# A block-triangular inverse by four-quadrant products in a state-space mixer, and merged small operations in a differential attention

## The chip, the cores and the metric

The kernel runs on one core of a Trainium2 chip. The core has a matrix engine (PE, TensorE), three engines for elementwise work (DVE is VectorE, ACT is ScalarE, POOL is GpSimd) and a queue that only issues transfers (SP). They share an on-chip memory (SBUF) and the matrix engine's output memory (PSUM, here two rings of four banks, `psum_a` and `psum_d`). The metric is the device time of one launch in microseconds (us), lower is better.

## The reference

The program is one block of a hybrid model (512 tokens, width 1024) followed by two layers of another. The change touches two places. The first block has an RWKV-7 mixer of 16 heads, whose state is updated token by token:

```python
def step(state, inp):
    r_t, w_t, k_t, v_t, a_t, b_t = inp
    sa = jnp.einsum('bhvk,bhk->bhv', state, a_t)
    state = (state * w_t[:, :, None, :] + sa[..., None] * b_t[:, :, None, :]
             + v_t[..., None] * k_t[:, :, None, :])
    return state, jnp.einsum('bhvk,bhk->bhv', state, r_t)
```

It is followed by a group norm per head (`(y - mu) * rsqrt(var + GN_EPS) * gn_w + gn_b`). Each of the two later layers has a differential attention of four heads; the output's squares belong to the norm behind it:

```python
s = s - slopes[None, None, :, None, None] * dist[:, None, None]
p = jax.nn.softmax(s, axis=-1)
a = p[:, 0] - lam * p[:, 1]
return jnp.einsum('bhqk,bkhd->bqhd', a.astype(v.dtype), v)
```

## The kernel before

Every engine runs a program written out by hand, in order; semaphores couple them. Semaphores `full_a`/`full_d` say that a PSUM bank is written, `free_a`/`free_d` that it was read out. ACT reads the ring `a`, DVE the ring `d`. Weights come as 440 blocks of 128x1024 through SP; POOL splits each block into two fp32r parts when PE has used the block before the last, so POOL works in bursts that follow PE's dense products (L574, L577, L578: three per 128x128 weight tile).

**The RWKV stage** runs from about 270 to 871 us. Eight iterations j = 0 to 7 (`pe_rwkv`, `act_rwkv`, `dve_rwkv`) take two heads each (a pair: 64 channels in the lower and 64 in the upper partitions) and four chunks of 128 tokens. In each chunk the recurrence is solved by the inverse of a unit triangular matrix of 128x128. The kernel builds the inverse by doubling. Its two diagonal blocks of 64x64, for eight units u (two heads times four chunks), lie in `R_TN`, and its transpose in `R_TC`. Level 0 gives both from masks. Then levels k = 1 to 5 each do:

- PE, helper `blocks` (L1195): Z = L · TN, 16 products of 64x64, whose input rows and output partitions are the same half; DVE multiplies by the level's mask (L2516);
- PE: `normal` = TC · Z (16 products), DVE adds it to `R_TN` (L2532);
- PE: `last` = the transposed update (16 products), DVE adds it to `R_TC` (L2532 again).

Between them stand the steps of the chain of the iteration before (`PeChain`): per chunk `first` (L1097, L1099, output W), `second` (L1112, L1114, output U = T · W), `third` (L1125 to L1134, new state and output Y). ACT copies W, U and Y out of PSUM (L1695), DVE makes the new state (L2456 to L2466). In levels 2 and 4 PE also computes dense products for the next iteration (24 instructions), in level 3 one plain product. DVE's own inputs for the next iteration are spread over the levels (`dve_rwkv_input`, the reciprocal L2414 in level 4), and the group norm of iteration j - 2 (`dve_rwkv_normed` with reciprocal L2564, `dve_rwkv_mixed`) stands in level 2. Level 5 is followed by transposes (L729), masked maps (`pe_rwkv_maps`, L1157 and L1159, DVE L2477) and the corner block (L1203) that joins the two diagonal blocks. DVE then prepares the next iteration (`dve_rwkv_prepare`, L2431 to L2444), for which PE waits at L637 (`rk_ready`).

**The differential attention** (two layers, about 1658 to 1741 and 2730 to 2813 us) has 32 units, two per pair. For each unit DVE adds distances and takes the row maximum (L2672), negates it (L2677), ACT takes the exponential with its sum (L1877); for each pair DVE takes two reciprocals (L2689, L2691) and combines both halves (L2693, L2696), PE transposes (L729), ACT copies (L1886), PE multiplies by V (L797), DVE scales the output (L2703) and sums its squares (L2706). PE fills with halves of gate products (L759, L762, L763).

## Time and profile before

| | us |
|---|---|
| time before, median of 3 runs | 3494.92 |
| the runs | 3494.77 to 3496.0 |
| the profiled execution's own time | 3495.8 |
| its span (first to last instruction) | 3494.0 |
| outside the span | 1.8 |
| granted PE clock, mean | 0.98 |

The granted clock is a share of 2.4 GHz; in a stretch it is either near 1 or near 0.5 (1.2 GHz). In a timeline row the record of a PE group overlaps the next one by its pipeline's tail, so what a group costs is read from start to start. An fp32 product stands as two matmul records, so 16 products are x32. A bracket at a row's end is the idle time of that engine ahead of it and what ended it.

### The profile page before, as it was taken

To read this page: it belongs to the slowest core of one execution; us is meant where nothing else is said; L and a number is where in the kernel's file an instruction comes from. 1 tells how busy PE (TensorE), PEld (TensorE's weight loads), DVE (VectorE), ACT (ScalarE), POOL (GpSimd) and SP (SyncE) were. 2 spreads that over 40 slices of the span, in tenths; PEclk is the share of its full clock that TensorE was granted. 3 is DMA by queue.
4 is the path that set the end of the run, shared out by engine and by line. 5 is a ranking of instruction groups with operands and counts; after the bars stand their busy time and mean duration, and the time that the engine had idled before them with its cause. 6 is when DMAs were issued, how large, how long until landed. Compare 5 with 4: busy or idle time off the path is not lost.

```text
span 3494.0 us, 54483 instructions
## 1 busy us (share of the span) xinstructions
PE 3296.9 (94%) x20334; PEld 2615.5 (75%) x20334; DVE 2061.9 (59%) x2829; ACT 1019.0 (29%) x1866; POOL 1679.5 (48%) x1323
## 2 busy tenths in 40 slices
PE   7988999999999999989899899999989999999999
PEld 4766777777888888657778788887657677788887
DVE  4647777874566555541745575557551645576556
ACT  2152322222121112551435231113462435231112
POOL 3423222222657664225264566665326363666665
PEclk9999999999999999999999999999999999999999
DMA  5431111111323332112021233332102121223332
...
DMA packets 71664, 268.48 MB, mean 77 GB/s; under 512 B 7840, under 2 KB 7968, under 8 KB 68384
## 3 DMA queue, kind: packets, MB, share of 16 engines
...
q14 instruction: 60, 0.49, 0.0%
...
## 4 chain that ended last, share of the span: by engine, by line
PE 74%; DVE 19%; ACT 3%; issue 2%; DMA 1%; DVEq 0%; POOL 0%; SPq 0%; ACTq 0%; POOLq 0%
PE psum_a L574 10%; PE psum_a L577 10%; PE psum_a L578 10%; PE psum_d L574 5%; PE psum_d L577 4%; PE psum_d L578 4%; PE psum_d L637 4%; PE psum_d L1195 3%; PE psum_a L729 2%; PE psum_a L600 2%; PE psum_d L832 2%; PE psum_a L604 2%; PE psum_a L603 2%; DVE arena L2672 1%; PE psum_a L759 1%
## 5 line engine op out<-in xcount | busy, mean ns | idle before, releaser
L3274 POOL TENSOR_TENSOR w_lo<-raw,w_hi 128x1024 fp32r<-128x1024 f32 x440 | 1119.4, 2544 | 36.7
L3270 POOL TENSOR_TENSOR mark<-mark 128x1 f32<-128x1 f32 x438 | 105.5, 241 | 1738.4 <-PE psum_a L574 899.3
L574 PE MATMUL psum_a<-h_hi,w_hi 128*128 128x512 f32 x1712 | 675.2, 394 | 0.0
L577 PE MATMUL psum_a<-h_lo,w_hi 128*128 128x512 f32 x1712 | 667.4, 390 | 0.0
L578 PE MATMUL psum_a<-h_hi,w_lo 128*128 128x512 f32 x1712 | 667.4, 390 | 0.0
L3271 POOL TENSOR_SCALAR w_hi<-raw 128x1024 fp32r<-128x1024 f32 x440 | 471.2, 1071 | 33.7 <-DMA raw<-in_weights 33.7
L574 PEld LDWEIGHTS psum_a<-h_hi,w_hi 128*128 128x128 f32 x1712 | 322.1, 188 | 77.8 <-issue 11.2
L578 PEld LDWEIGHTS psum_a<-h_hi,w_lo 128*128 128x128 f32 x1712 | 322.0, 188 | 67.7
L577 PEld LDWEIGHTS psum_a<-h_lo,w_hi 128*128 128x128 f32 x1712 | 322.0, 188 | 67.4 <-issue 1.9
L574 PE MATMUL psum_d<-split,w_hi 128*128 128x512 f32 x848 | 331.2, 391 | 9.5 <-DVE x L3021 6.7
L577 PE MATMUL psum_d<-split,w_hi 128*128 128x512 f32 x848 | 330.0, 389 | 0.0
L578 PE MATMUL psum_d<-split,w_lo 128*128 128x512 f32 x848 | 330.0, 389 | 0.0
L574 PEld LDWEIGHTS psum_d<-split,w_hi 128*128 128x128 f32 x848 | 159.2, 188 | 47.2 <-issue 13.0
L578 PEld LDWEIGHTS psum_d<-split,w_lo 128*128 128x128 f32 x848 | 159.2, 188 | 33.1
L577 PEld LDWEIGHTS psum_d<-split,w_hi 128*128 128x128 f32 x848 | 159.2, 188 | 32.7
L637 PE MATMUL psum_d<-arena 64*128 64x512 f32 (+4 forms) x480 | 158.1, 566 | 12.1 <-DVEq L2819 6.9
L1195 PEld LDWEIGHTS psum_d<-arena 64*64 64x64 f32 x3840 | 123.9, 137 | 40.0 <-issue 14.2
L1195 PE MATMUL psum_d<-arena 64*64 64x64 f32 x3840 | 138.1, 224 | 15.2 <-DVE arena L2532 10.9
L759 PE MATMUL psum_a<-h_hi,w_hi 128*128 128x256 f32 x416 | 123.7, 297 | 0.0
L1841 ACT ACTIVATE arena<-arena,col 128x512 f32<-128x512 f32 (+5 forms) x144 | 104.3, 725 | 47.1 <-DVE col L2610 26.4
L763 PE MATMUL psum_a<-h_hi,w_lo 128*128 128x256 f32 x416 | 117.6, 283 | 0.0
L762 PE MATMUL psum_a<-h_lo,w_hi 128*128 128x256 f32 x416 | 117.6, 283 | 0.0
...
## 6 DMA issues: line engine op xcount, KB each, us to landing
raw<-in_weights SPq DMA_DIRECT2D x440, 512.0 KB, 3.6
...
```

Of the source, the lines that this page charges most:

```text
L574: m = pe.eng.matmul(dst, wh, hi(t), start=t == 0, stop=False)
L577: pe.eng.matmul(dst, wh, lo(t), start=False, stop=False)
L578: m = pe.eng.matmul(dst, wl, hi(t), start=False, stop=t == k - 1)
L637: pe.eng.matmul(tl.ps[0:lhsT.shape[1], 0:rhs.shape[1]], lhsT, rhs, start=True, stop=True)\
L759: m = pe.eng.matmul(tl.ps[:, cols], wh, b.h_hi[:, t, cols], start=t == 0, stop=False)
L762: pe.eng.matmul(tl.ps[:, cols], wh, b.h_lo[:, t, cols], start=False, stop=False)
L763: m = pe.eng.matmul(tl.ps[:, cols], wl, b.h_hi[:, t, cols], start=False, stop=t == KD - 1)
L1195: m = pe.eng.matmul(tl.ps[r, u * HD:(u + 1) * HD], lhsT(r, u), rhs[r, u], start=True, stop=True)
L1841: a.eng.activation(u.x, u.x, ACT.Exp, bias=u.neg, scale=1.0 if u.scale is None else u.scale, accum_out=u.sum)\
L3270: eng.tensor_tensor(b.mark[:, 1:2], b.mark[:, 0:1], b.mark[:, 0:1], ALU.add)
L3271: eng.tensor_scalar(hi, b.raw[:, s], 1.0, 0.0, ALU.mult, ALU.add).then_inc(sig["w_high"], 1)
L3274: eng.tensor_tensor(lo, b.raw[:, s], hi.bitcast(F32), ALU.subtract).then_inc(sig["w_ready"], 1)
```

## The change

- `products` takes the place of `blocks`: again 16 products of 64x64 per call, but a step through all four combinations of input half and output half, into two banks of ring `d`. The output blocks lie transposed against the input, so that Z is written with halves exchanged, and the second call brings them back.
- `R_TC` and its update are gone. Each level transposes `R_TN` (four 128x128 transposes, `inverse`), ACT copies it to `R_TW`, and the second product reads that. `diagonal` (16 products with the identity) gives the transposed diagonal blocks once, behind level 5.
- DVE's mask and add become two instructions each of half width (one per bank), 2 x 128x4x64.
- `second` of the chain reads one 128x128 matrix `R_TF` (its lower left zeroed in iterations 0 and 1): two products instead of four.
- In level 5 the second product stands ahead of the transposes and maps.
- `dve_rwkv_normed` of iteration j - 2 stands ahead of the levels, no longer in level 2.
- In the differential attention one negation and one reciprocal serve both units of a pair, ACT waits for `s_ready` once a pair, and the sum of squares is done by ACT (`act_output_square`).

```diff
         self.R_LM = ar(21, 8).rearrange("p (u m t) -> p u m t", u=8, m=4)
         self.R_Z, self.R_TN = (ar(a).rearrange("p (u t) -> p u t", u=8) for a in (29, 30))
-        self.R_TC = [ar(a).rearrange("p (u t) -> p u t", u=8) for a in (31, 32)]
-        self.R_T6 = [ar(a).rearrange("p (u t) -> p u t", u=8) for a in (33, 34)]
+        self.R_TW = self.plain[:, 6].rearrange("p (u t) -> p u t", u=8)
+        self.R_TF = [ar(a, 2).rearrange("p (u t) -> p u t", u=8) for a in (31, 33)]
         self.R_E = (self.col[:, 156:159], self.col[:, 172:175])
         self.R_WU = ar(35, width=1024).rearrange("p (s n) -> p s n", s=8)
         self.R_Y, self.R_YC, self.R_SQ, self.R_STD = (ar(n) for n in (37, 38, 41, 42))
...
         pe.eng.wait_ge(self.w.free, pe.taken(self.w))
         tl = pe.tile("a")
         pe.eng.wait_ge(tl.free, pe.emptied(tl))
-        upper, lower = ROWS
         for r, u in self.heads(c):
-            pe.eng.matmul(tl.ps[upper, r], self.TC[upper, u], self.W[upper, r], start=True, stop=True)
-        for r, u in self.heads(c):
-            m = pe.eng.matmul(tl.ps[lower, r], self.T6[:, u], self.W[:, r], start=True, stop=True)
+            m = pe.eng.matmul(tl.ps[:, r], self.TF[:, u], self.W[:, r], start=True, stop=True)
         m.then_inc(tl.full, pe.up("full_a"))
         self.u = tl
...
-    def blocks(lhsT, rhs):
+    def products(lhsT, rhs):
+        tiles = [pe.tile("d") for _ in range(2)]
+        pe.eng.wait_ge(tiles[1].free, pe.emptied(tiles[1]))
+        for v in range(4):
+            for n, (row, out) in enumerate(((0, 0), (1, 1), (0, 1), (1, 0))):
+                m = pe.eng.matmul(tiles[row].ps[ROWS[out], v * HD:(v + 1) * HD], lhsT(v, row, out), rhs(v, row, out),
+                                  start=True, stop=True)
+                if v == 3 and n >= 2:
+                    m.then_inc(tiles[row].full, pe.up("full_d"))
+        return tiles[1]
+
+    def block(t, v, row, out):
+        return t[ROWS[row], 2 * v + out]
+
+    def diagonal(src):
         tl = pe.tile("d")
         pe.eng.wait_ge(tl.free, pe.emptied(tl))
         for u in range(8):
             for r in ROWS:
-                m = pe.eng.matmul(tl.ps[r, u * HD:(u + 1) * HD], lhsT(r, u), rhs[r, u], start=True, stop=True)
+                m = pe.eng.matmul(tl.ps[r, u * HD:(u + 1) * HD], src[r, u], b.ident[r, r], start=True, stop=True)
         m.then_inc(tl.full, pe.up("full_d"))
         return tl
...
         else:
             pe.eng.wait_ge(normal.free, pe.taken(normal))
-        z = blocks(lambda r, u: LT[r, u, r], b.R_TN)
+        z = products(lambda v, row, out: LT[ROWS[row], 2 * v + out, ROWS[row]], lambda *at: block(b.R_TN, *at))
+        inverse = pe_turned(pe, [b.R_TN[:, 2 * v:2 * v + 2].rearrange("p u t -> p (u t)") for v in range(4)])
         if c is not None:
             chain.first(c)
         if k == 2 and more:
@@ -1222,27 +1234,26 @@
         if k == 5:
             if j:
                 pe_rwkv_mean(pe)
+        pe.eng.wait_ge(inverse.free, pe.taken(inverse))
+        pe.eng.wait_ge(z.free, pe.taken(z))
+        normal = products(lambda *at: block(b.R_TW, *at), lambda *at: block(b.R_Z, *at))
+        if k == 5:
             for src in (b.R_V, b.R_BH, b.R_KH):
                 turned = pe_turned(pe, [src[:, q * P:(q + 1) * P] for q in range(NQ)])
             pe_rwkv_maps(pe, j, (0, 1))
-        if k == 1:
-            pe.eng.wait_ge(pe.sem["t_ready"], pe.due("t_ready"))
-        pe.eng.wait_ge(z.free, pe.taken(z))
-        normal = blocks(lambda r, u: TC[r, u], b.R_Z)
         if c is not None:
             chain.second(c)
-        last = blocks(lambda r, u: b.R_Z[r, u], TC)
-        if c is not None:
             chain.third(c)
         if k == 3 and more:
             pe_rwkv_length(pe)
     upper, lower = ROWS
     pe.eng.wait_ge(normal.free, pe.taken(normal))
     z = corner(lower, lambda u: LT[upper, u, lower], lambda u: b.R_TN[upper, u])
+    last = diagonal(b.R_TN)
     maps = pe_rwkv_maps(pe, j, (2, 3))
     pe.eng.wait_ge(last.free, pe.taken(last))
     pe.eng.wait_ge(z.free, pe.taken(z))
-    last = corner(upper, lambda u: b.R_Z[lower, u], lambda u: b.R_T6[j % 2][lower, u])
+    last = corner(upper, lambda u: b.R_Z[lower, u], lambda u: TF[lower, u, HD:])
     if j:
         pe_rwkv_variance(pe)
     return PeChain(pe, j, (turned, maps, last))
...
@@ -1708,7 +1719,12 @@
     else:
         a.eng.wait_ge(a.sem["rk_ready"], KD)
         act_late_gate(a, 0)
-    for k in range(1, NQ + 1):
+    for k in range(1, NQ + 2):
+        a.eng.wait_ge(a.sem["full_a"], a.due("full_a"))
+        a.eng.activation(b.R_TW, a.bank().rearrange("p (u t) -> p u t", u=8), ACT.Copy).then_inc(a.sem["free_a"], a.up("free_a"))
+        if k > NQ:
+            continue
         if j:
             act_rwkv_chunk(a, W)
...
@@ -1869,7 +1885,8 @@
         if 0 <= s - 1 < n_units:
             u = units[s - 1]
-            a.eng.wait_ge(a.sem["s_ready"], a.due("s_ready"))
+            if s % 2:
+                a.eng.wait_ge(a.sem["s_ready"], a.due("s_ready"))
             if u.sink is not None:
                 a.eng.activation(u.sunk, u.sink, ACT.Exp, bias=u.neg).then_inc(a.sem["act_step"], a.up("act_step"))
@@ -1885,6 +1902,18 @@
                 a.eng.activation(u.pt[:, b0 * P:b0 * P + w], a.bank()[:, 0:w], ACT.Copy)\
                     .then_inc(a.sem["free_a"], a.up("free_a"))
+        if 0 <= s - lag - 3 and units[s - lag - 3].v:
+            act_output_square(a, units[s - lag - 3])
+    for u in units[-2:]:
+        if u.v:
+            act_output_square(a, u)
+
+
+def act_output_square(a, u):
+
+    a.eng.wait_ge(a.sem["o_written"], a.due("o_written"))
+    a.eng.activation(u.square[0], u.o, ACT.Square, accum_out=u.square[1]).then_inc(a.sem["act_step"], a.up("act_step"))
...
@@ -2225,6 +2253,9 @@
         u.inv, u.sunk = b.col[:, 124 + n % 4:125 + n % 4], b.col[:, 128 + n % 8:129 + n % 8]
         if u.neg_lam is not None:
             u.inv = b.col[:, n % 32:n % 32 + 1]
+        if n % 2:
+            u.two_top, u.two_inv = b.col[:, 119 + n % 4:121 + n % 4], b.col[:, n % 32 - 1:n % 32 + 1]
+            u.two_neg, u.two_sum = b.col[:, c - 2:c + 2:2], b.col[:, c - 1:c + 3:2]
     return units
...
+    eight, four = (lambda ps: ps.rearrange("p (u t) -> p u t", u=8)), (lambda ps: ps[:, 0:4 * HD].rearrange("p (v t) -> p v t", v=4))
+    every = lambda t, half: t.rearrange("p (v i) t -> p v i t", i=2)[:, :, half]
     for us in (slice(0, 4), slice(4, 8)):
         v.eng.wait_ge(v.sem["full_d"], v.due("full_d"))
@@ -2504,20 +2536,17 @@
             .then_inc(v.sem["free_d"], v.up("free_d"))
     v.eng.tensor_tensor(b.R_TN, b.R_TN, eye, ALU.add).then_inc(v.sem["t_ready"], v.up("t_ready"))
-    for r in ROWS:
-        v.eng.tensor_tensor(TC[r], b.R_LM[r, :, 0, r], low1t[r], ALU.mult).then_inc(v.sem["dve_step"], v.up("dve_step"))
-    v.eng.tensor_tensor(TC, TC, eye, ALU.add).then_inc(v.sem["t_ready"], v.up("t_ready"))
+    if j >= 2:
+        dve_rwkv_normed(v, j - 2)
     for k in range(1, 6):
-        level = v.each(b.const[:, C_LEVEL + (k - 1) * HD:C_LEVEL + k * HD], 8)
-        v.eng.wait_ge(v.sem["full_d"], v.due("full_d"))
-        v.eng.tensor_tensor(b.R_Z, eight(v.bank()), level, ALU.mult).then_inc(v.sem["free_d"], v.up("free_d"))
+        level = v.each(b.const[:, C_LEVEL + (k - 1) * HD:C_LEVEL + k * HD], 4)
+        for half in range(2):
+            v.eng.wait_ge(v.sem["full_d"], v.due("full_d"))
+            v.eng.tensor_tensor(every(b.R_Z, half), four(v.bank()), level, ALU.mult).then_inc(v.sem["free_d"], v.up("free_d"))
         if k == 2 and more:
             dve_rwkv_input(v, j + 1, 2)
         if k == 2 and j >= 2:
-            dve_rwkv_normed(v, j - 2)
             dve_rwkv_mixed(v, j - 2)
         if k == 4 and more:
             for step in (4, 8, 9):
@@ -2525,22 +2554,26 @@
         if k == 5:
             if j:
                 dve_rwkv_centered(v)
-            dve_rwkv_maps(v, (0, 1))
-        for dst in (b.R_TN, TC) if k < 5 else (b.R_TN,):
+        for half in range(2):
+            dst = every(b.R_TN, half)
             v.eng.wait_ge(v.sem["full_d"], v.due("full_d"))
-            v.eng.tensor_tensor(dst, dst, eight(v.bank()), ALU.add).then_inc(v.sem["free_d"], v.up("free_d"))
+            v.eng.tensor_tensor(dst, dst, four(v.bank()), ALU.add).then_inc(v.sem["free_d"], v.up("free_d"))
         if k == 5:
-            v.eng.wait_ge(v.sem["full_d"], v.due("full_d"))
-            ps, step = eight(v.bank()), "dve_step"
-            for r, dst in zip(ROWS, (TC, b.R_T6[j % 2])):
-                v.eng.tensor_tensor(dst[r], TC[r], ps[r], ALU.add).then_inc(v.sem[step], v.up(step))
-                step = "free_d"
+            dve_rwkv_maps(v, (0, 1))
         if j and k < NQ:
             dve_rwkv_state(v, j - 1, k - 1)
         if k in (1, 3) and more:
             dve_rwkv_input(v, j + 1, k)
+    if j < 2:
+        v.eng.memset(TF[HD:P, :, 0:HD], 0.0).then_inc(v.sem["dve_step"], v.up("dve_step"))
+    v.eng.wait_ge(v.sem["full_d"], v.due("full_d"))
+    ps, step = eight(v.bank()), "dve_step"
+    for r, cols in zip(ROWS, ROWS):
+        v.eng.tensor_copy(TF[r, :, cols], ps[r]).then_inc(v.sem[step], v.up(step))
+        step = "free_d"
     dve_rwkv_maps(v, (2, 3))
     if more:
         dve_rwkv_input(v, j + 1, 7)
@@ -2672,23 +2705,15 @@
                 v.eng.tensor_tensor_reduce(out=u.s[:, at:at + w], in0=v.bank()[:, 0:w], in1=m, scale=1.0, scalar=least, op0=ALU.add, op1=ALU.max, accum_out=u.top)\
                     .then_inc(v.sem["free_d"], v.up("free_d"))
                 at, least = at + w, u.top
-            if u.scale is None or u.dist is not None:
-                v.eng.tensor_scalar(u.neg, u.top, -1.0 if u.scale is None else -u.scale, None, ALU.mult)\
-                    .then_inc(v.sem["s_ready"], v.up("s_ready"))
-            else:
-                v.eng.tensor_scalar(u.neg, u.top, -1.0, u.scale, ALU.mult, ALU.mult)\
-                    .then_inc(v.sem["s_ready"], v.up("s_ready"))
-            if extra:
-                extra(s)
+            if s % 2:
+                v.eng.tensor_scalar(u.two_neg, u.two_top, -u.scale, None, ALU.mult).then_inc(v.sem["s_ready"], v.up("s_ready"))
         if 0 <= s - 2 < len(us) and us[s - 2].ready == "p_ready" and us[s - 2].v:
             u0, u1 = us[s - 3], us[s - 2]
             if base + s - 1 > 0:
                 v.eng.wait_ge(v.sem["e_done"], v.value("e_done", base + s - 1))
-            v.eng.reciprocal(u0.inv, u0.sum).then_inc(v.sem["dve_step"], v.up("dve_step"))
-            v.eng.reciprocal(u1.inv, u1.sum).then_inc(v.sem["dve_step"], v.up("dve_step"))
+            v.eng.reciprocal(u1.two_inv, u1.two_sum).then_inc(v.sem["dve_step"], v.up("dve_step"))
             v.eng.scalar_tensor_tensor(u1.inv, u1.inv, u1.neg_lam, u0.sum, ALU.mult, ALU.mult)\
...
@@ -2703,8 +2728,7 @@
                 v.eng.tensor_scalar(u.o, v.bank()[:, 0:u.width], us[s - lag - 2 - late_by].inv, None, ALU.mult)\
                     .then_inc(v.sem["free_d"], v.up("free_d"))
-                v.eng.tensor_tensor_reduce(out=u.square[0], in0=u.o, in1=u.o, scale=1.0, scalar=0.0, op0=ALU.mult, op1=ALU.add, accum_out=u.square[1])\
-                    .then_inc(v.sem["dve_step"], v.up("dve_step"))
+                v.eng.sem_inc(v.sem["o_written"], v.up("o_written"))
             else:
                 if u.sink is not None:
```

The engine PE in a middle iteration with a chain, level 1 up to its dense products. L1195 is `blocks`, L1099 `first`, L1112 and L1114 `second`, L1125 to L1134 `third`. Before:

```order
L1195 MATMUL psum_d<-arena 64x64 x16
L1099 MATMUL psum_a<-arena 128x64 x2
L1195 MATMUL psum_d<-arena 64x64 x16
L1112 MATMUL psum_a<-arena 64x64 x2
L1114 MATMUL psum_a<-arena 64x64 x2
L1195 MATMUL psum_d<-arena 64x64 x16
L1125 MATMUL psum_d<-arena 128x128
```

After, where L1192 is `products`, L729 the transposes of `inverse`, L1111 `second` and L1122 the start of `third`:

```order
L1192 MATMUL psum_d<-arena 64x64 x16
L729 MATMUL psum_a<-const,arena 128x128 x4
L1099 MATMUL psum_a<-arena 128x64 x2
L1192 MATMUL psum_d<-arena,plain 64x64 x16
L1111 MATMUL psum_a<-arena 128x64 x2
L1122 MATMUL psum_d<-arena 128x128
```

The third group of 16 between `second` and `third` is gone, four transposes stand behind the first group, and `second` has two instructions for four.

The engine DVE from the end of level 0 to level 1, iterations j >= 2. L2506 adds the unit diagonal to `R_TN`, L2509 and L2511 build `R_TC`. Before:

```order
L2506 TENSOR_TENSOR arena<-arena,const 128x512
L2509 TENSOR_TENSOR arena<-arena,const 64x512 x2
L2511 TENSOR_TENSOR arena<-arena,const 128x512
L2516 TENSOR_TENSOR arena<-psum_d,const 128x512
L2532 TENSOR_TENSOR arena<-arena,psum_d 128x512 x2
```

After, where L2597 and L2599 are `dve_rwkv_normed`:

```order
L2538 TENSOR_TENSOR arena<-arena,const 128x512
L2597 RECIPROCAL arena<-arena 128x512
L2599 SCALAR_TENSOR_TENSOR arena<-arena,par 128x512
L2546 TENSOR_TENSOR arena<-psum_d,const 128x4x64 x2
L2561 TENSOR_TENSOR arena<-arena,psum_d 128x4x64 x2
```

The reciprocal takes the place of the transposed copy's setup; mask and add are two halves each, and the second add is gone.

The engine DVE in level 2 of the same iterations: mask, shift of the next keys (L2729, L2731), group norm, add. Before:

```order
L2516 TENSOR_TENSOR arena<-psum_d,const 128x512
L2729 TENSOR_TENSOR arena<-arena 128x512
L2731 SCALAR_TENSOR_TENSOR arena<-arena,par 128x512
L2564 RECIPROCAL arena<-arena 128x512
L2566 SCALAR_TENSOR_TENSOR arena<-arena,par 128x512
L2574 SCALAR_TENSOR_TENSOR arena<-arena,par 128x512
L2577 TENSOR_TENSOR plain<-arena 128x512
L2532 TENSOR_TENSOR arena<-arena,psum_d 128x512 x2
```

After:

```order
L2546 TENSOR_TENSOR arena<-psum_d,const 128x4x64 x2
L2753 TENSOR_TENSOR arena<-arena 128x512
L2755 SCALAR_TENSOR_TENSOR arena<-arena,par 128x512
L2607 SCALAR_TENSOR_TENSOR arena<-arena,par 128x512
L2610 TENSOR_TENSOR plain<-arena 128x512
L2561 TENSOR_TENSOR arena<-arena,psum_d 128x4x64 x2
```

Between the mask and the add stand four instructions where six stood.

## Rows read from the trace of the kernel before

**Rows 1.** The page, part 1: busy us, share of the span, count, by engine.

```profile
PE 3296.9 (94%) x20334; PEld 2615.5 (75%) x20334; DVE 2061.9 (59%) x2829; ACT 1019.0 (29%) x1866; POOL 1679.5 (48%) x1323
```

**Rows 2.** Windows, iteration 3: length, busy PE, PEld, DVE, ACT, POOL; PE clock, DMA.

```profile
483.50:554.30 70.80, 64.93 (x828) 52.72 (x827) 56.39 (x70) 20.81 (x41) 21.30 (x16) 0.99 0.13 39
```

**Rows 3.** Timeline of PE in iteration 3: start, length, engine, line, operation, output and inputs.

```profile
485.55 0.69 PE L1181 MATMUL psum_d<-arena 64*64 64x64 f32 x32
...
495.19 1.15 PE L1195 MATMUL psum_d<-arena 64*64 64x64 f32 x32 [0.25 <-issue]
496.46 0.45 PE L1114 MATMUL psum_a<-arena 128*64 128x64 f32 x4
496.84 1.15 PE L1195 MATMUL psum_d<-arena 64*64 64x64 f32 x32
497.92 0.49 PE L1125 MATMUL psum_d<-arena 128*128 128x128 f32 x2
...
532.53 1.47 PE L729 MATMUL psum_a<-const,arena 128*128 128x128 f32 x12
```

**Rows 4.** Timeline of DVE and of ACT in iteration 3: a half-width pair, two PSUM copies.

```profile
487.24 0.95 DVE L2503 TENSOR_TENSOR arena<-psum_d,const 128x256 f32<-128x256 f32 x2
...
496.95 0.28 ACT L1695 ACTIVATE arena<-psum_a 128x128 f32<-128x128 f32 x1 [1.70 <-PE psum_a L1114]
...
533.17 1.98 ACT L1731 ACTIVATE arena<-psum_a 128x512 f32<-128x512 f32 x3 [2.27 <-PE psum_a L729]
```

**Rows 5.** Waits of PE from 270 to 900 us: total, times, longest.

```profile
PE psum_d L637 <- DVE col L2444: 19.2, 7, 4.8
PE psum_d L1195 <- DVE arena L2532: 10.9, 8, 3.7
PE psum_a L1097 <- DVE arena L2462: 6.0, 7, 2.0
```

**Rows 6.** Timeline, PE and DVE: levels 3 to 5 in iterations 3 and 5.

```profile
511.30 1.15 PE L1195 MATMUL psum_d<-arena 64*64 64x64 f32 x32 [0.44 <-DVE arena L2532]
...
519.28 1.15 PE L1195 MATMUL psum_d<-arena 64*64 64x64 f32 x32
...
528.29 0.69 DVE L2532 TENSOR_TENSOR arena<-arena,psum_d 128x512 f32<-128x512 f32 x1
...
530.49 1.15 PE L1195 MATMUL psum_d<-arena 64*64 64x64 f32 x32
...
654.56 1.32 PE L1195 MATMUL psum_d<-arena 64*64 64x64 f32 x32 [1.78 <-DVE arena L2532]
...
665.05 1.15 PE L1195 MATMUL psum_d<-arena 64*64 64x64 f32 x32
...
676.88 1.48 DVE L2532 TENSOR_TENSOR arena<-arena,psum_d 128x512 f32<-128x512 f32 x2
...
677.62 0.56 PE L1195 MATMUL psum_d<-arena 64*64 64x64 f32 x12 [1.29 <-DVE arena L2532]
```

**Rows 7.** Timeline: a DVE line that prepares iterations 3 and 4, PE in 4.

```profile
479.15 0.69 DVE L2437 TENSOR_TENSOR arena<-arena 128x512 f32<-128x512 f32 x1
...
546.94 2.77 DVE L2437 TENSOR_TENSOR arena<-arena 128x512 f32<-128x512 f32 x1
...
554.30 2.07 PE L637 MATMUL psum_d<-arena,const 128*128 128x512 f32 x2 [3.75 <-DVE col L2444]
```

**Rows 8.** Differential attention, layer 0: a PE wait (total, times, longest), then timeline rows.

```profile
PE psum_d L797 <- ACT arena L1886: 7.4, 10, 1.8
...
1725.58 0.29 DVE L2706 CUSTOM_DVE_ANT_0 plain<-arena 128x128 f32<-128x128 f32 x1
...
1738.94 1.28 ACT L2052 ACT_TABLE_LOAD   x1
...
1741.56 2.29 DVE L2947 TENSOR_TENSOR arena<-arena,col 128x2048 f32<-128x2048 f32 x1
...
1745.41 1.91 PE L729 MATMUL psum_a<-const,arena 128*128 128x128 f32 x16
```

26 lines of the change are left out of this document (11 added, 15 removed).

## The prediction

> **What bounds the kernel now.** I read the page first: PE is busy for 94% of the span, DVE for 59% [rows 1]. So an edit pays only where it takes work or a wait from PE. Then the windows of the iterations of the RWKV stage, which is where nearly all of the change lies: the middle one takes 70.80 us with PE busy for 64.9, its clock at 0.99 and DVE busy for 56.4 [rows 2]. PE is the bound, but DVE is close behind, and each gain of PE has to be checked against what DVE delivers at that point. Third, PE's timeline through one level of the inverse [rows 3], with the DVE and ACT instructions between the products [rows 4]. Fourth, PE's waits in the stage, 36 us on three DVE lines [rows 5], and where they fall [rows 6, 7]. Last the differential attention [rows 8].
>
> **PE's work in one level (1 to 4).** Before, from start to start: Z 1.08 (the same group as 496.84 to 497.92), `normal` and `second` together 495.19 to 496.84 = 1.65, `last` 1.08; sum 3.81 [rows 3]. After:
> - Each call of `products` has the form of L1181, which walks the four combinations of halves too: its record is 0.69 where that of L1195 is 1.15 [rows 3], and less the same overlap of 0.07 that is 0.62. Two calls: 1.24. The other end is 1.08 a call, if the new order of combinations doesn't overlap.
> - Four transposes: a third of L729's twelve, (1.47 - 0.07) / 3 = 0.47 [rows 3].
> - `second` with two instructions: the lower half alone costs 0.38 now (496.46 to 496.84) [rows 3].
> - A new wait. `last` stood between `second` and `third` and covered ACT's copy of U. Without it PE stands until that copy is done: `second` ends at 496.84, the copy runs from 496.95 for 0.28 [rows 3, 4], and the next product can start some 0.05 later: 0.44.
>
> Sum 1.24 + 0.47 + 0.38 + 0.44 = 2.53, so 1.28 less per level. In levels 1 and 3 the second product also waits for `R_TW`: transposes done at 1.09, an ACT copy of 128x512 takes 1.98 / 3 = 0.66 [rows 4], ready at about 1.9 after Z's start, when PE is out of other work (0.62, 0.47 and `first`). I take 0.3 in each, an estimate, and give back the 0.25 that PE waits in level 1 today [rows 3]: -0.3 per iteration. Halving DVE's mask costs 0.95 for two [rows 4] against 0.69 [rows 6]; this stays below `R_TW`'s path. Three levels in the seven iterations with a chain: 7 x (3 x 1.28 - 0.3) = **24.8**.
>
> **Level 4 belongs to DVE.** It runs the inputs of the next iteration there (with a reciprocal), and only then the add to `R_TN`. In iteration 3 this add ends 9.70 after the level's start (519.28 to 528.98) and PE goes on at 11.21; in iteration 5 it ends at 12.5 and PE waits 1.29 [rows 6]. These are the ends of six iterations. New, PE could go on at 9.9. DVE's way to the add is the same: the masks start 0.46 earlier, the halves of mask and add cost 0.5 more. So iterations 3 and 7 gain 1.28, iteration 6 about 1.0, iteration 1 0.3, the others nothing: **3.9**.
>
> **Waits that go.** `dve_rwkv_normed` leaves level 2 (more than 4 us of DVE) and takes the place of `R_TC`'s setup, which had cover from dense products and ended ahead of the first mask. So the wait for the add ahead of level 3 goes, 4.4 of L2532's 10.9 us in four iterations, from 0.44 to 1.78 [rows 5, 6]; and with one add fewer ahead of the state, L2462's wait in level 3, 3.2 of 6.0 [rows 5]. **7.6**. After the two largest of these pairs the clock was at its lower level: level 3 of iteration 5 takes 654.56 to 665.05 = 10.49 [rows 6] where the same work takes 7.98 (511.30 to 519.28) at full clock in iteration 3; iteration 2 loses 1.5 in the same way: **4.2**.
>
> **The rest of the stage.** Level 5 to the next L637: PE loses `normal` and `last` behind the maps but gains `diagonal` (1.08), and its last two maps now wait for the bank that DVE frees with the copy into `R_TF`. The masked maps end 0.3 earlier at most. PE's 19.2 us at L637 stay [rows 5]: the preparing instructions are the same. I put 0.15 per iteration, **1.2**. Iteration 0 has no chain, its levels run product, DVE, product; about 0.4 per level: **1.7**. The chain behind the last iteration has its `second` shortened by 0.32 four times: **1.3**.
>
> **Differential attention.** Per pair DVE loses a negation, a reciprocal and a sum of squares (0.29 and its readout [rows 8]), some 0.75 us. PE gains little. Its wait is for ACT's copy of the transposed weights, 7.4 us in layer 0 in ten waits [rows 8], and in ACT's order that copy stands behind the exponential of the pair's first unit, which now comes one row maximum later. Only the start, with four row maxima in a chain, is shorter, 0.8 a layer. At the end the table load (1.28) now stands behind the last square; the output is scaled at 1743.85 and PE takes it at 1745.41 [rows 8], so 1.28 fits. **1.6** for both layers.
>
> **New losses.** In iterations 2 and 5 PE will stand for some 2.6 us ahead of level 5 (1.2 today), and after such waits the clock was low; and `dve_rwkv_normed` has instructions with two SBUF inputs, which are stretched while POOL works (0.69 against 2.77 for one line [rows 7]). **-4.0**.
>
> **Sum.** 24.8 + 3.9 + 7.6 + 4.2 + 1.2 + 1.7 + 1.3 + 1.6 - 4.0 = 42.3. The profiled execution took 3495.8, so 3453.5; the median of the runs is 0.9 lower, so **3453**. The change adds no transfer and moves none.
>
> **Rivals.**
> - *The four combinations don't overlap in the new order.* Then each call costs 1.08. Levels 1 to 3 lose 0.92 each: 7 x 3 x 0.92 = 19.3, and level 4 some 2: 3474. For it: L1181 takes its halves in another order. Against: its inputs alternate in the same way, and its banks are laid out alike. The Trainium skill (TensorEngine Tiling (Array Packing), section Instruction Overhead) puts about 60 cycles on every matmul and advises against taking a tiling factor from a dimension that is small already; by that rule 64x64 blocks would gain nothing from four quadrants and this rival's time would hold. L1181's row speaks against it.
> - *DVE holds more than level 4.* PE arrives 2.8 us earlier at level 2's add as well. If POOL's bursts meet DVE's two shift instructions and the two of `dve_rwkv_mixed` at 2 us each, level 2 gains nothing in most iterations, and the front of level 1 waits: some 12 less: 3465. Rows 7 show how large a stretch is; that it comes in each iteration speaks against. The Trainium skill (SBUF — State Buffer, section SBUF: two separate sides) says that a VectorE instruction with two SBUF inputs and a GpSimd instruction shut each other out for a whole instruction; the two lengths of L2437 agree.
> - *More of it reaches the end.* If the bursts fall elsewhere in level 4 (5 us) and PE's 7.4 us of waits in each attention [rows 8] shrink by half, and no new low clock comes (4): 3453 - 16 = 3437.
> - *Slower: the clock.* PE now stands 0.44 in each level and a little more for `R_TW`, where before it ran through. After 3.75 us of waiting PE's next product took 2.07, twice its length [rows 7], and after 1.78 the level was stretched. If gaps of half a microsecond in a row have the same effect, each level's 4.2 us of short products (2.1 of the sum above, as much for `first` and `third`) take twice that: 28 levels x 4.2 = 118, 3571. It decides from ten levels on (42.3 / 4.2). Against: in iteration 3 a gap of 0.44 [rows 6] was followed at once by one of L2462's, 0.86 in the mean [rows 5], and level 3 ran at full clock.
> - *No measurable change*: several of the terms above fail at once.
>
> **How the numbers follow.** Forecast 0.55 (its own range 3440 to 3464), the first rival 0.10, DVE 0.14, more 0.13, slower 0.04, no change 0.04. A range of 3432 to 3472 holds the forecast, DVE's case, two thirds of "more", and some of the first rival: 0.8. Faster by over 0.2% (what a measurement here can tell from no change, 7 us) 0.92, within 0.04, slower 0.04.
>
> **What will show it.** `products` records of 0.69 and not 1.15; a wait of about 0.44 at `third` on ACT's L1695 counterpart, 28 times; no waits ahead of level 3; waits of 1 to 2.7 ahead of level 5; L637's wait near 19; iterations some 5 to 6 us shorter than before; the attention stages within 2 us of their old length. The prediction is wrong if PE's clock falls in the levels, if level 2 waits for DVE, or if the attention stages move by more than 3 us.

## The result and the profile after

| | us |
|---|---|
| before, median of 4 runs | 3494.85 (3494.34 to 3496.0) |
| changed, median of 4 runs | 3470.47 (3468.71 to 3470.57) |
| ratio | 0.9929, 95% interval 0.9916 to 0.9941 |
| span of the profiled execution, before and after | 3494.0 and 3468.5 |

The change saves 24 us; forecast were 42 (range 3432 to 3472, which 3470 just meets). The mechanism was right in the RWKV stage, which gained nearly what was forecast, though partly because errors of its terms cancel; in the differential attention, of which I expected a small gain, the right mechanism was seen and its price left out, and 8.5 us were lost. That the time lies in the range is owed to the range's width. The page of the changed kernel, part 1, answers to [rows 1]:

```profile
PE 3250.9 (94%) x19342; PEld 2564.8 (74%) x19342; DVE 2011.6 (58%) x2727; ACT 1056.0 (30%) x1970; POOL 1673.7 (48%) x1323
```

**Where the time went.** I matched the same products of both traces and read the distance between them. The stage runs from the first L637 of iteration 0 (276.66 before, 276.20 after) to that of the last iteration's output (871.15 and 831.61). Each attention is taken from the last block of products with weights ahead of it to the first behind it (the L574 at 1624.84 and 1747.08 before, 1586.78 and 1713.40 after). The last row of the table ends with the last product that both traces have.

| stretch, us | before | after | difference | forecast |
|---|---|---|---|---|
| RWKV stage | 594.49 | 555.41 | -39.1 | -40.7 |
| behind it, to attention 1 | 753.69 | 755.17 | +1.5 | 0 |
| attention 1 | 122.24 | 126.62 | +4.4 | -0.8 |
| between the attentions | 949.63 | 951.94 | +2.3 | 0 |
| attention 2 | 122.46 | 126.60 | +4.1 | -0.8 |
| behind it | 669.39 | 671.07 | +1.7 | 0 |

With the 0.5 us ahead of the stage these make the 25.5 us between the spans. So two things are to be explained: 10 us in the attentions and 5.5 in stretches where both kernels have the same instructions.

**The stage.** The window of iteration 3 (length, busy PE, PEld, DVE, ACT, POOL, clock, DMA), against 70.80 us in [rows 2]:

```profile
473.54:535.98 62.44, 58.34 (x704) 45.71 (x702) 50.72 (x73) 23.79 (x46) 18.47 (x15) 1.00 0.13 43
```

PE's timeline through level 1 of the same iteration, against [rows 3]:

```profile
483.23 0.69 PE L1192 MATMUL psum_d<-arena 64*64 64x64 f32 x32
483.86 0.66 PE L729 MATMUL psum_a<-const,arena 128*128 128x128 f32 x4
484.35 0.56 PE L1099 MATMUL psum_a<-arena 128*128 128x64 f32 x4
485.20 0.69 PE L1192 MATMUL psum_d<-arena,plain 64*64 64x64 f32 x32 [0.29 <-ACT plain L1725]
485.83 0.66 PE L1111 MATMUL psum_a<-arena 128*128 128x64 f32 x4
486.85 0.49 PE L1122 MATMUL psum_d<-arena 128*128 128x128 f32 x2 [0.37 <-ACT arena L1706]
...
488.09 0.69 PE L1192 MATMUL psum_d<-arena 64*64 64x64 f32 x32
```

This is the forecast, row for row: a call of `products` is recorded with 0.69 and costs 0.63 (483.23 to 483.86), the transposes 0.49, the wait for `R_TW` 0.29, that for U 0.37 where I had 0.44. The level takes 4.86 us; it took 5.95 (493.20 to 499.15 before). PE's waits of the stage (270 to 900 us; engine, line waited for, total, times, longest), against [rows 5]:

```profile
PE psum_d L1192 <- DVE arena L2561: 15.9, 8, 5.7
PE psum_d L637 <- DVE col L2475: 11.3, 6, 4.8
PE psum_d L1154 <- DVE arena L2575: 8.1, 8, 1.8
PE psum_d L1122 <- ACT arena L1706: 7.7, 21, 0.4
PE psum_d L1192 <- ACT plain L1725: 3.7, 8, 0.7
...
PE psum_a L1128 <- ACT arena L1706: 2.6, 7, 0.4
```

L2561 is the add to `R_TN`, L2475 the end of `dve_rwkv_prepare`, L2575 the copy into `R_TF`, L1706 the chain's copy. The 28 waits for U (7.7 + 2.6) are there; at the last maps PE now stands 8.1 us for the bank that the copy into `R_TF` frees, where before it stood 4.9 in front of the corner block. The two things that the forecast did not have are in DVE's timeline. The first is iteration 7, level 1, here before (ahead of the level, which starts at 779.28) and after (it starts at 743.37), with POOL's instruction of that time:

```profile
775.65 2.76 DVE L2506 TENSOR_TENSOR arena<-arena,const 128x512 f32<-128x512 f32 x1
...
780.68 0.69 DVE L2516 TENSOR_TENSOR arena<-psum_d,const 128x512 f32<-128x512 f32 x1
```

```profile
739.73 2.75 DVE L2538 TENSOR_TENSOR arena<-arena,const 128x512 f32<-128x512 f32 x1
742.59 3.35 DVE L2597 RECIPROCAL arena<-arena 128x512 f32<-128x512 f32 x1
745.98 0.75 DVE L2599 SCALAR_TENSOR_TENSOR arena<-arena,par 128x512 f32<-128x512 f32 x1
746.83 0.95 DVE L2546 TENSOR_TENSOR arena<-psum_d,const 128x256 f32<-128x256 f32 x2
```

```profile
739.54 2.40 POOL L3296 TENSOR_TENSOR w_lo<-raw,w_hi 128x1024 fp32r<-128x1024 f32 x1
```

The add of the diagonal (L2538) takes 2.75 us for its usual 0.69 while POOL's L3296 runs, but that is not new: it took 2.76 before. New is what stands behind it, the norm's 4.1 us where the setup of `R_TC` took 2.1. So the mask comes 3.46 us after the level's start and not 1.40, and PE stands 2.85 us ahead of its second product at 747.89; the level takes 9.3 us for 4.9. Iteration 6 loses 0.7: there the add takes 0.69, and the norm's second instruction is stretched from 0.75 to 2.82 beside the same line of POOL:

```profile
680.25 2.82 DVE L2599 SCALAR_TENSOR_TENSOR arena<-arena,par 128x512 f32<-128x512 f32 x1
```

The second is the end of iteration 3, before and after (last two instructions of the preparation):

```profile
550.47 1.56 DVE L2442 TENSOR_TENSOR arena<-arena 128x512 f32<-128x512 f32 x1
552.07 2.18 DVE L2444 TENSOR_TENSOR col<-arena,col 128x3 f32<-128x3 f32 x1
```

```profile
534.17 0.69 DVE L2473 TENSOR_TENSOR arena<-arena 128x512 f32<-128x512 f32 x1
534.90 1.03 DVE L2475 TENSOR_TENSOR col<-arena,col 128x3 f32<-128x3 f32 x1
```

The same two instructions take 3.7 us before and 1.7 after. POOL's next burst begins at 550.18 before, ahead of the first of the two, and its long instruction runs beside the second; after, the burst begins at 534.18, when the first has just started, and the second ends at 535.93, ahead of the long one. These are POOL's rows before:

```profile
550.18 0.31 POOL L3270 TENSOR_TENSOR mark<-mark 128x1 f32<-128x1 f32 x1 [1.02 <-PE psum_d L574]
550.45 1.04 POOL L3271 TENSOR_SCALAR w_hi<-raw 128x1024 fp32r<-128x1024 f32 x1
551.58 2.65 POOL L3274 TENSOR_TENSOR w_lo<-raw,w_hi 128x1024 fp32r<-128x1024 f32 x1
```

PE waits 2.3 us less at L637 in this iteration. No run moved POOL's bursts, so that they are the cause is read from these times and not tested.

**The attention.** PE's waits in the first one (1586.78 to 1713.40), against 7.4 us in [rows 8], and ACT's timeline of a pair:

```profile
PE psum_d L797 <- ACT arena L1903: 11.1, 9, 2.2
```

```profile
1641.13 0.72 ACT L1894 ACTIVATE plain<-arena,col 128x512 f32<-128x512 f32 x1
...
1643.42 0.72 ACT L1894 ACTIVATE plain<-arena,col 128x512 f32<-128x512 f32 x1 [0.98 <-DVE col L2710]
1644.05 0.19 ACT L1894 ACTIVATION_READ_ACCUMULATOR plain<-arena,col 128x1 f32 x1
1644.33 0.60 ACT L1903 ACTIVATE arena<-psum_a 128x512 f32<-128x512 f32 x1
1644.95 0.72 ACT L1894 ACTIVATE plain<-arena,col 128x512 f32<-128x512 f32 x1
```

L2710 is the merged negation. The pair's first exponential (1643.42) waits for it, and the copy that PE needs for L797 (L1903) stands behind that exponential.

### The profile page after: what moved, and what is told of

Its sections match the earlier page's. It is cut to its first block, busy times and chain, and to the rows that moved or that the text cites. A ratio compares the mean times of both kernels' runs of the same rounds, so it can differ in the third digit from the quotient of the medians.

```text
span 3468.5 us, 52617 instructions
## 1 busy us (share of the span) xinstructions
PE 3250.9 (94%) x19342; PEld 2564.8 (74%) x19342; DVE 2011.6 (58%) x2727; ACT 1056.0 (30%) x1970; POOL 1673.7 (48%) x1323
## 4 chain that ended last, share of the span: by engine, by line
PE 77%; DVE 16%; ACT 4%; issue 2%; DMA 1%; POOL 0%; SPq 0%; DVEq 0%; ACTq 0%; POOLq 0%
PE psum_a L574 10%; PE psum_a L578 10%; PE psum_a L577 10%; PE psum_d L637 5%; PE psum_d L574 5%; PE psum_d L578 5%; PE psum_d L577 5%; PE psum_a L729 3%; PE psum_a L600 2%; PE psum_d L832 2%; PE psum_a L603 2%; PE psum_a L604 2%; PE psum_d L1192 1%; PE psum_a L759 1%; PE psum_a L763 1%
## 5 line engine op out<-in xcount | busy, mean ns | idle before, releaser
L3296 POOL TENSOR_TENSOR w_lo<-raw,w_hi 128x1024 fp32r<-128x1024 f32 x440 | 1114.6, 2533 | 36.7
L574 PE MATMUL psum_a<-h_hi,w_hi 128*128 128x512 f32 x1712 | 676.6, 395 | 0.0
L574 PEld LDWEIGHTS psum_a<-h_hi,w_hi 128*128 128x128 f32 x1712 | 323.0, 189 | 77.8 <-issue 11.2
L574 PE MATMUL psum_d<-split,w_hi 128*128 128x512 f32 x848 | 331.2, 391 | 9.5 <-DVE x L3043 6.7
L574 PEld LDWEIGHTS psum_d<-split,w_hi 128*128 128x128 f32 x848 | 159.1, 188 | 47.1 <-issue 13.1
L637 PE MATMUL psum_d<-arena 64*128 64x512 f32 (+4 forms) x480 | 158.5, 579 | 12.2 <-DVEq L2843 6.9
L729 PE MATMUL psum_a<-const,arena 128*128 128x128 f32 x820 | 117.7, 283 | 2.8 <-DVEq L2972 1.6
L729 PEld LDWEIGHTS psum_a<-const,arena 128*128 128x128 f32 x820 | 93.1, 143 | 31.2 <-issue 20.0
```

The costliest lines, as they stand in the source:

```text
L574: m = pe.eng.matmul(dst, wh, hi(t), start=t == 0, stop=False)
L637: pe.eng.matmul(tl.ps[0:lhsT.shape[1], 0:rhs.shape[1]], lhsT, rhs, start=True, stop=True)\
L729: m = pe.eng.transpose(tl.ps[:, q * P:(q + 1) * P], s, pe.b.ident)
L3296: eng.tensor_tensor(lo, b.raw[:, s], hi.bitcast(F32), ALU.subtract).then_inc(sig["w_ready"], 1)
```

## The experiments

All times are medians; "stage" and "attention" are the lengths of the table above, read from each trace. Time lost to the clock is, here and below, the sum over windows of 10 us of length times (1 - mean granted clock). A low clock while PE waits counts in it and costs nothing: ahead of the stage the two traces of before lose 8.6 and 15.4 us and reach it within 0.1 us of each other. Every run of before beside them lay between 3493.4 and 3498.3.

| kernel | median, us | ratio to before, 95% interval | stage | attention 1, 2 |
|---|---|---|---|---|
| changed | 3470.47 | 0.9929 (0.9916 to 0.9941) | 555.4 | 126.6, 126.6 |
| attention_back | 3457.35 | 0.9892 (0.9875 to 0.9908) | 555.6 | 121.9, 122.1 |
| negation_back | 3460.18 | 0.9895 (0.9879 to 0.9912) | 555.6 | 120.4, 120.4 |
| squares_back | 3477.65 | 0.9944 (0.9928 to 0.9961) | 558.8 | 127.7, 126.6 |
| copy_first | 3453.33 | 0.9883 (0.9866 to 0.9899) | 552.7 | 119.3, 119.0 |
| two_quadrants | 3489.74 | 0.9981 (0.9971 to 0.9990) | 576.5 | 126.6, 126.6 |
| norm_in_level2 | 3482.28 | 0.9959 (0.9945 to 0.9973) | 566.5 | 126.6, 126.6 |
| copy_covered | 3461.43 | 0.9902 (0.9886 to 0.9919) | 545.2 | 126.6, 126.6 |
| steps_moved | 3455.78 | 0.9888 (0.9872 to 0.9905) | 541.1 | 126.6, 126.6 |
| after_again | 3470.32 | 0.9930 (0.9914 to 0.9947) | 555.6 | 126.6, 126.6 |
| before_again | 3496.13 | 1.0002 (0.9992 to 1.0011) | 594.5 | 122.2, 122.2 |
| best | 3438.34 | 0.9837 (0.9820 to 0.9853) | 534.7 | 120.4, 120.5 |
| best_copy_first | 3432.69 | 0.9820 (0.9804 to 0.9837) | 538.8 | 118.9, 118.9 |

**The attention: whole, then by parts.** attention_back restores all of the attention's code. negation_back restores this alone:

```
-            if s % 2:
-                a.eng.wait_ge(a.sem["s_ready"], a.due("s_ready"))
+            a.eng.wait_ge(a.sem["s_ready"], a.due("s_ready"))
...
-            if s % 2:
-                v.eng.tensor_scalar(u.two_neg, u.two_top, -u.scale, None, ALU.mult)
+            v.eng.tensor_scalar(u.neg, u.top, -u.scale, None, ALU.mult)
```

> The changed kernel with the differential attention of the kernel before (a negation and a wait per unit, two reciprocals, the sum of squares on DVE); the RWKV stage as changed. Theory A (the attention's edits lose time: in the changed kernel PE arrives 38.06 us earlier than before ahead of the first attention and 33.67 us behind it, 31.37 and 27.23 around the second, 8.5 us in all): about 3462 us, and both attentions again as long as before. Rival B (the attention is as long only because the work falls otherwise against POOL's bursts, and these follow from the earlier arrival): no gain, 3468 to 3472. Rival C (the attention gained the 1.6 us of the forecast and the loss lies elsewhere): 3472. Short stretches at the lower clock can move either by 2 us.

> The changed kernel with only the merged negation undone: DVE negates each unit's row maximum and ACT waits for each; the merged reciprocal and the squares on ACT stay. Theory A1 (the merged negation makes the pair's first exponential wait for the second row maximum, 0.87 us later, and ACT's copy of the transposed weights stands behind that exponential, so PE's waits at the product with V grow from 0.60 to 1.49): the 3.4 and 3.1 us lost inside the pairs of the two layers come back, about 3464 us. Theory A2 (the squares on ACT are to blame, 0.50 us of ACT per unit ahead of the next copy): no more than 1 us comes back, 3469 to 3471.

squares_back takes the sum of squares from ACT to DVE again (`tensor_tensor_reduce` behind the scaling for `act_output_square`):

> The changed kernel with only the sum of squares given back to DVE; merged negation and reciprocal stay. Theory A1 (the negation is to blame for the loss in the pairs, the squares for the 1.0 us behind each attention, where the square root's table load stands behind the last square): 2 us come back, about 3468 us. Theory A2 (the squares are to blame for all): 8 us come back, about 3462 us.

Measured: the attentions of attention_back are 4.8 and 4.5 us shorter than the changed ones, so A holds, B and C fall. With the negation alone restored they are 6.2 us shorter, twice what A1 had, and 1.8 and 2.0 shorter than before. So the merged reciprocal and the squares on ACT are worth some 2 us a layer, and the merged negation costs 6. (Its median is still 2.8 us above that of attention_back: in its trace the stage starts 2.7 later and the stretches with unchanged instructions take 6 us more.) With the squares back on DVE the first attention is 1.0 longer and the second as long: A2 falls. What A1 had for the squares is not shown either way, since this trace alone has low clock in the attentions (1.7 and 3.4 us lost); even with all of that added back, 4.1 us would have come back of A2's 8. Its median, 7 us above the changed kernel's, is not an effect of the squares: in its trace 3.4 us are in the stage and 3.1 in the stretches outside stage and attentions, where its instructions are those of the changed kernel (see "Twice the same kernel").

The cause inside the negation: copy_first keeps it merged and only changes ACT's order in each step (gate halves and copy ahead of the exponential).

```
+        act_gate_halves(a, s % 2 * halves_at(s // 2, n_units // 2, gates))
+        if 0 <= s - lag < n_units and units[s - lag].v:
+            u = units[s - lag]
...
         if 0 <= s - 1 < n_units:
             u = units[s - 1]
...
-        act_gate_halves(a, s % 2 * halves_at(s // 2, n_units // 2, gates))
-        if 0 <= s - lag < n_units and units[s - lag].v:
```

> The changed kernel with the merged negation kept, and in each step of ACT's attention loop the gate halves and the copy of the transposed weights ahead of the exponential. Theory A1 (the merged negation costs time because that copy stands in ACT's order behind an exponential that waits for the second row maximum): PE's waits at the product with V fall from 11.1 us per layer to 4 or less, and the attentions get 6 us shorter each, as in negation_back: 3458. Rival A3 (the exponential itself is what the next pair waits for, whatever stands ahead of it): no gain, 3470, or a loss, since the exponential now waits for PE's transposes.

PE's waits in its first attention, and those of negation_back:

```profile
PE psum_d L797 <- ACT arena L1892: 2.5, 3, 1.1
```

```profile
PE psum_d L797 <- ACT arena L1902: 5.4, 7, 1.4
```

11.1 us became 2.5 with the negation still merged, and the attentions are 7.4 and 7.6 us shorter, 3.0 and 3.5 us shorter than in the kernel before: A3 falls. That shows the mechanism: not the negation as such, but the copy's place behind an exponential that waits for it. (2.7 us more of this run's gain lie in the stage, which it does not touch; there its trace loses 5 us less to the clock.)

**The quadrants.**

```
-        for v in range(4):
-            for n, (row, out) in enumerate(((0, 0), (1, 1), (0, 1), (1, 0))):
+        for v, n in [(v, n) for ns in ((0, 1), (2, 3)) for v in range(4) for n in ns]:
```

> The changed kernel with another order inside each call of the products: for all four v first the two combinations whose input and output half agree, then the two others, so that only two of the four quadrants alternate at a time. Theory Q (four quadrants overlap because four different ones follow each other; with two the call costs 1.08 us as in the kernel before and not 0.62): 80 calls, of which those of level 4 are partly hidden, at 0.46 us: some 33 us more, 3500 to 3507. Rival R (what counts is that each call has 16 products of this size, the order is nothing): 3470.

The record of a call is now 0.98 (this row stands for the 0.69 at 483.23), and the next group starts 0.90 later:

```profile
493.31 0.98 PE L1193 MATMUL psum_d<-arena 64*64 64x64 f32 x32
494.21 0.66 PE L729 MATMUL psum_a<-const,arena 128*128 128x128 f32 x4
```

The stage is 21.1 us longer, 80 calls at 0.27 less what level 4 hides; the loss to the clock in it, 25.5, is that of the changed kernel. The run's ten times spread from 3483.1 to 3494.3. The order within a call decides, R falls; but the price of two alternating quadrants is 0.90 and not the 1.08 of the kernel before. What makes up the 0.18 between them was not tried (before, both combinations write one bank, here two).

**The norm's place.** `dve_rwkv_normed` back in level 2:

> The changed kernel with the group norm's reciprocal and scaling back in level 2, where they stood before, ahead of DVE's add. Theory N (that place is what PE waited for at level 3, 7.6 us in the kernel before, and PE now arrives 2 us earlier in each of the six iterations): 7.6 + 6 x 0.9 = 13 us more, 3483, and waits ahead of level 3 in the profile. Rival O (these waits went because one add fewer stands in the level, wherever the norm is): 3470 to 3473.

```profile
PE psum_d L1192 <- DVE arena L2560: 25.0, 13, 5.7
```

Waits for the add ahead of level 3 are back in iterations 2 to 6 (3.11, 1.95, 1.97, 3.16 and 1.14 us), the stage is 11.0 longer; the loss to the clock in it rises from 25.6 to 30.6. Theory N holds. In iterations 6 and 7 level 1 is short again (4.9 us each), so the waits shown above for the changed kernel are the norm's price there. The 11.0 are a balance: levels 2 and 3 take 22.9 us more, level 1 gives back 5.3 and the rest of the iterations 6.6.

**The wait for U.**

```
-        if c is not None:
+        if c == 0:
             chain.first(c)
+        inverse = pe_turned(pe, [b.R_TN[:, 2 * v:2 * v + 2].rearrange("p u t -> p (u t)") for v in range(4)])
+        if c:
+            chain.first(c)
...
+        if c in (0, 1, 3):
+            chain.second(c)
         pe.eng.wait_ge(inverse.free, pe.taken(inverse))
...
-        if c is not None:
+        if c == 2:
             chain.second(c)
```

> The changed kernel in another order on PE and ACT: in levels 1, 2 and 4 the chain's second product stands ahead of the level's second product, which then covers ACT's copy of U, and in level 1 the chain's first product and its copy stand ahead of the transposes. Theory U (PE stands 0.37 us in each level for the copy of U, 10.3 us in 28 waits in the profile, and 0.3 us for the copy of the transposed inverse in level 1): 7 x (0.37 + 0.37 + 0.3) = 7.3 us in levels 1 and 2, and in level 4, where DVE sets the end in half of the iterations, some 1.3 more: about 3462 us. Rival V (DVE's adds come later by the 0.31 us of the moved product, and DVE is what PE waits for in the end): 3468 to 3471 with the 10 us of waits for the copy turned into waits for DVE's adds.

(On ACT the copy of W stands ahead of that of the transposes in level 1.) The stage is 10.2 us shorter. The waits for U fall from 10.3 to 5.6 us and those for DVE's add rise from 15.9 to 18.2:

```profile
PE psum_d L1192 <- DVE arena L2568: 18.2, 10, 5.6
...
PE psum_d L1122 <- ACT arena L1711: 4.6, 13, 0.4
```

U holds; V took 2.3 us of it. The expectation of the gain (8.6 us) came out, but half of what was gained is the clock's, which it did not have: the stage loses 20.5 us to it for 25.6, although the waits ahead of level 5 are longer here.

**Level 4 and the clock.** In the changed kernel the clock was low in these stretches of the stage (windows cut around them; the third figure from a row's end is the mean granted clock):

```profile
384.00:390.00 6.00, 5.60 (x82) 3.95 (x82) 2.73 (x6) 1.20 (x2) 0.00 (x0) 0.72 0.15 61
450.00:458.00 8.00, 6.48 (x82) 4.62 (x82) 3.64 (x8) 1.23 (x3) 0.00 (x0) 0.57 0.19 68
578.00:584.00 6.00, 4.98 (x76) 3.34 (x77) 2.83 (x7) 0.60 (x1) 0.00 (x0) 0.72 0.23 83
644.00:648.00 4.00, 2.93 (x38) 2.19 (x38) 1.69 (x4) 0.60 (x1) 0.00 (x0) 0.57 0.00 0
```

They begin at PE's waits for level 4's add: 1.03 us ahead of 384.40, 2.56 ahead of 451.52, 1.70 ahead of 579.02, 2.55 ahead of 645.07. steps_moved shortens those waits only, by two multiplications that DVE now does behind the adds:

```
-            for step in (4, 8, 9):
+            for step in (4, 8):
...
+        if k == 4 and more:
+            dve_rwkv_input(v, j + 1, 9)
```

(step 9 here holds the product that makes `R_KK`, too)

> The changed kernel with only the two multiplications of level 4 moved behind the level's adds on DVE. In the profile of the run best the RWKV stage is 10.5 us shorter than in copy_covered, and 10.2 us of that is the clock (20.5 us of full-clock time lost to the lower level in the stage against 10.3). Theory W (the waits of 1.0 to 2.6 us ahead of level 5 are what the clock falls after; without them it stays up): waits ahead of level 5 under 1.5 us outside iteration 0, the stage 5 us shorter by the waits and some 5 more by the clock, the stretches at the lower clock at 384, 450, 578 and 644 us gone: 3460. Rival X (the clock's fall has nothing to do with these waits): 5 us by the waits alone, 3465, and as many low stretches as in the changed kernel.

The waits ahead of level 5 fall by 8.6 us and the same places run at full clock:

```profile
PE psum_d L1192 <- DVE arena L2561: 7.3, 4, 4.2
```

```profile
376.00:392.00 16.00, 14.18 (x218) 10.91 (x216) 12.03 (x17) 4.77 (x9) 3.58 (x3) 1.00 0.12 35
436.00:460.00 24.00, 21.86 (x268) 16.96 (x266) 19.62 (x28) 7.93 (x16) 3.56 (x3) 1.00 0.08 24
560.00:590.00 30.00, 28.27 (x294) 21.96 (x294) 25.07 (x34) 9.93 (x17) 7.74 (x6) 1.00 0.06 19
```

The stage is 14.3 us shorter, its loss to the clock 15.4 for 25.6. X falls: these low stretches go with the waits. 1.7 us came back behind the stage in a new one.

For these four places W holds, with exceptions. In the six traces with the changed kernel's stage (after, its repetition, attention_back, negation_back, squares_back, copy_first) 23 of the 24 waits, 1.03 to 2.56 us long, are met by low clock, copy_first's 1.03 is not; in copy_covered, where they are 1.41 to 2.94, two of four are; in the three kernels with the multiplications moved, none of the places is.

The size of the clock's part is less firm than one trace makes it look. The same stage instructions lose 25.6 us in the changed kernel, 28.9 in squares_back and 20.6 in copy_first, and those of best and best_copy_first, below, lose 10.3 and 20.5 and take 534.7 and 538.8. In best the waits of 3.2 and 2.2 us in iterations 5 and 7 leave the clock up, in best_copy_first the same two bring it down.

**Twice the same kernel.**

> The changed kernel once more, on the chip of the runs beside it, for a second trace of the same program. Theory D (the stretches at the lower clock outside the RWKV stage, such as the 3.4 us at 1355 that cost 1.6, come at the same places in each execution, so they belong to the program): the trace agrees with the first to 1 us at every dense block, 3470.5. Rival E (they fall anew in each execution and on each chip): the two traces drift apart by 1 to 3 us at blocks in which the program is the same, and the median lies between 3466 and 3474.

> The kernel before once more, for a second trace of it. Outside the RWKV stage and the two attentions the traces of before and after differ by 5.5 us against the changed kernel. Theory E (the short stretches at the lower clock fall anew in each execution; the second trace of the changed kernel drifted 4.4 us from the first and came back to -1.2): this trace drifts by 2 to 5 us from the first of before, too, at blocks in which nothing differs, and its loss to the clock outside the stage, 49.8 us in the first trace, lies nearer the 50 to 60 of the changed kernels. Rival D (the drift belongs to the program): it agrees with the first trace to 1 us everywhere.

The two traces of before agree to 0.3 us at every block, so for before rival D holds. The two of the changed kernel do not: the second arrives 4.4 us later than the first at attention 1 (0.7 at the stage's start, 1.0 at its end) and ends 1.2 earlier. Over all fourteen traces the three stretches with the same instructions outside stage and attentions take, together, 2372.7 us (before, both times) to 2381.3 (squares_back); the changed kernel has 2378.2 and 2376.0. Before is at the low end. The time lost to the clock behind the stage goes with it: 39.6 us in before, 45.9 and 43.0 in the two traces of the changed kernel. With the loss inside the three stretches taken off each trace, 2332 to 2336 us are left in all fourteen, 2334.1 in before and 2333.3 in the changed kernel. So the 5.5 us are the clock's, in low stretches that move when the work ahead of them moves (one of the changed kernel's, at 1354 to 1358, costs 1.6 us in a block that runs at full clock before). Why they fall where they fall stays open; nothing in the diff touches these places. The start of the stage moves in the same way, from 276.2 to 279.6 us over the fourteen traces.

**Together.** best has copy_covered, negation_back and steps_moved in one kernel; best_copy_first adds copy_first's order.

> The changed kernel with the order of the run copy_covered, the negation per unit of the run negation_back, and on DVE two multiplications of level 4 (the scaled keys and their product with the rates) behind the level's adds, where DVE stands idle for 0.99 us ahead of the next mask. Theory: the gains add up, 9.6 us of copy_covered and 12.4 of negation_back by their traces, and level 4's adds end 1.4 us earlier, of which four iterations use 1.0 to 1.4 and iteration 0 all: some 5 us more: 3470.5 - 9.6 - 12.4 - 5 = 3443.5. Rival (the adds' place moves the wait into level 5: the mask comes later and PE waits there): 3449.

> The run best (negation per unit, the chain's second product early, two multiplications behind the adds) with the same order of ACT's attention loop, copies ahead of the exponential. Theory A1 gives a part of the 5.4 us that PE still waits for the copy in each layer: 3438.3 - 6 = 3432. Rival A3: the exponential comes later and DVE with it, 3438 to 3445.

Both came out shorter than or at their forecast: 3438.3 and 3432.7, 1.6% and 1.8% below before and 32 and 38 us below the changed kernel. In the stage best loses only 10.3 us to the clock, best_copy_first 20.5 with the same instructions; of the 5.7 us between their medians the attentions explain 3.1. In best PE waits 3.2 us for the mask, in six waits, the small part of the rival that came true.

## Why the prediction was right or wrong

- **PE's work in a level**: right. 0.63 for a call (0.62), 0.37 for U (0.44), 0.29 for `R_TW` (0.3). Level 2, free of disturbance, is 1.17 us shorter (11.64 to 10.47 in iteration 1), level 3 1.09. Levels 1 to 3 of seven iterations sum to 29.6 us less; the terms 24.8, 7.6 and 4.2 had 36.6. Five of the seven missing are level 1 of iterations 6 and 7, where the norm stands in front (41.9 us became 39.3 in the seven level 1, not the 34.2 of an undisturbed one). The step that failed is that `R_TC`'s setup "had cover" and that the norm, twice as long, would have it too: in iteration 7 the add ahead of it already took 2.76 us and PE already waited 0.46 for the mask before the change. The norm's stretched instruction was named among the new losses, in a term of 4.0 that had to serve for the clock, too.
- **Waits ahead of level 3**: right. The run with the norm back has them again, and its stage is 11.0 us longer, 5.0 of it lost to the clock; the forecast had 7.6 for the waits (3.2 of them another's, L2462's) and 4.2 for the clock.
- **Level 4 is DVE's**: right in kind, 2.8 us for 3.9. Waits ahead of level 5 were to be 1 to 2.7: they are 1.03, 2.56, 0, 1.70, 2.55, 0.29.
- **The rest of the stage**: the levels of iteration 0 gained 1.3 for 1.7. From level 5 to the next level 1, seven times, it is 1.7 in sum. Behind the last level 5 it is 3.8 for 1.3, and 1.7 of that is a low stretch that went.
- **L637's waits stay**: wrong, 11.3 for 19.2. The step that failed is "the preparing instructions are the same": they are the same instructions, and 2 us shorter where POOL's burst no longer meets them. Of the 7.9 us, 4.6 are no gain: in iteration 0 PE lost the same time to the clock ahead of them (25.75 us from level 5 to L637 for 25.74).
- **Half-clock stretches go, new ones come**: the places were right (levels 3 of iterations 2 and 5 run at full clock, the waits ahead of level 5 bring new ones), the balance was not: the stage loses 25.6 us to the clock for 22.1 before. By their places, 10.2 us of low stretches went (the forecast had 4.2) and 13.7 came, 8.5 of them at the waits for level 4's add. The term of 4.0 for new losses was too small. This and the norm's front nearly cancel against the gains at L637 and behind it, which is why the stage's 39.1 looks better than its terms are.
- **Differential attention, 1.6 gained**: wrong, 8.5 lost, and this is the miss. The prediction had the mechanism in its own words ("that copy stands behind the exponential of the pair's first unit, which now comes one row maximum later") and drew "PE gains little" from it where a loss follows: PE waits for that copy, so its delay of 0.87 us a pair, bounded by the pairs in which PE waits, is a price. The counts of removed DVE instructions were no gain since DVE was not what PE waited for. The runs priced the merged negation at +6.2 a layer, reciprocal and squares together at -1.9.
- **Rest of the program unchanged**: wrong by 5.5 us for a reason that could not be read from the trace of before. The range had no term for it.
- **Rivals**: that the combinations don't overlap fell; the order does matter, as two_quadrants shows. The Trainium skill (TensorEngine Tiling (Array Packing), section Instruction Overhead) puts about 60 cycles on a matmul and advises against a tiling factor from a small dimension. What I drew from it, that 64x64 blocks would gain nothing from four quadrants, does not hold here: 0.63 against 0.90 us for the same 16 products. The clock did not fall in the levels for gaps of 0.3 to 0.4 us: iteration 3 ran at 1.00.
- **Its own signs of being wrong**: one was met in full, the attentions moved by 4.4 and 4.1 us, more than the 3 that I had set. The clock did fall in levels 1 to 3 too, but in iteration 7 alone, at the wait of 2.85 us that the norm causes and not at the short gaps. Level 2's add kept PE waiting for no more than 0.22 us from iteration 1 on.
